# Taking sixteen experts in turn over four groups, and giving the rows before and after them to VectorE

## What is computed

```
h2   = rmsnorm(x1, g) * (1 + scale2) + shift2          # 320 x 2048
g    = top-1 of 4 expert groups;  e1, e2 = top-2 of the 4 experts of that group
out  = sum over the two:  weight * (silu(h2 @ w_gate[e]) * (h2 @ w_up[e])) @ w_down[e]
y    = rmsnorm(x1 + gate2 * out)
```

## Time and profile before

| | us |
|---|---|
| median of 3 runs | 1412.45 |
| range of the runs | 1411.66 to 1415.14 |
| the profiled execution's own time | 1411.79 |
| its span in the profile | 1409.8 |
| reciprocal root done, h2 begins | 745.8 |
| first expert's first product | 806.6 |
| last product of the last expert | 1355.9 |
| last VectorE instruction | 1405.1 |

### The profile page before, as it was taken

The page is one execution under the profiler, slowest core; times in us unless marked ns, Lnnn a source line. Parts: engine busy times, 40 slices in busy tenths (PEclk is TensorE's granted clock), DMA queues, the critical chain, the costliest instruction groups (busy, mean ns, idle before and its releaser), DMA issues.

```text
span 1409.8 us, 15927 instructions
## 1 busy us (share of the span) xinstructions
PE 1180.1 (84%) x6268; PEld 620.0 (44%) x6269; DVE 313.4 (22%) x624; ACT 200.7 (14%) x386; POOL 119.5 (8%) x129
## 2 busy tenths in 40 slices
PE   2678999999999999999991399999987877788740
PEld 0235665645445445444440344444644444444420
DVE  0101221142132232121109410111112111111128
ACT  2002111022022222100102000110211111111102
POOL 2010000000000001000007000000000000000016
PEclk9777999999999999999995599999999999999975
DMA  9987787766566439633512468877999999999953
GB/s 333 421 349 258 308 319 276 298 268 271 204 258 255 179 138 344 238 144 130 212 76 75 181 255 315 309 280 301 382 406 414 413 409 398 402 412 413 423 201 112
DMA packets 71717, 401.07 MB, mean 284 GB/s; under 512 B 6490, under 2 KB 6714, under 8 KB 39646
## 3 DMA queue, kind: packets, MB, share of 16 engines
q1 hardware_dynamic: 63216, 368.59, 66.8%
q0 software_dynamic: 6944, 23.99, 5.2%
q10 hardware_dynamic: 1520, 7.98, 1.4%
HBM read 394.85 MB, written 17.22 MB: 292 GB/s over the span
## 4 chain that ended last, share of the span: by engine, by line
PE 65%; DMA 26%; DVE 6%; issue 1%; ACT 1%; POOL 0%; SPq 0%; POOLq 0%; DVEq 0%
PE bank L825 20%; DMA arena<-in_w_up_dram 18%; PE bank L902 10%; PE bank L1175 8%; PE bank L829 5%; PE bank L817 5%; DMA arena<-in_w_ada_dram 5%; PE bank L1172 5%; PE bank L1198 4%; DMA arena<-in_w_gate_dram 2%; PE bank L1195 1%; PE bank L846 1%; DVE arena L1499 1%; PE bank L1036 1%; PE bank L1158 1%
## 5 line engine op out<-in xcount | busy, mean ns | idle before, releaser
L825 PE MATMUL bank<-arena 128*128 128x512 f32 x640 | 283.4, 596 | 0.0
L1172 PE MATMUL bank<-arena 128*64 128x256 f32 x1536 | 187.6, 403 | 58.3 <-DMA arena<-in_w_gate_dram 31.7
L825 PEld LDWEIGHTS bank<-arena 128*128 128x128 f32 x640 | 118.6, 190 | 137.7 <-issue 136.5
L1172 PEld LDWEIGHTS bank<-arena 128*64 128x64 f32 x1536 | 113.6, 145 | 137.0 <-DMA arena<-in_w_gate_dram 43.0
L902 PE MATMUL bank<-arena 128*128 128x320 f32 x512 | 143.2, 440 | 3.8 <-DVE arena L1274 3.8
L817 PE MATMUL bank<-arena 128*32 128x512 f32 x768 | 102.4, 674 | 45.0 <-DMA arena<-in_w_ada_dram 33.2
L902 PEld LDWEIGHTS bank<-arena 128*128 128x128 f32 x512 | 97.9, 192 | 51.1 <-issue 7.8
L1175 PE MATMUL bank<-arena 128*128 128x512 f32 x256 | 112.0, 598 | 6.9 <-issue 6.9
L1195 PE MATMUL bank<-arena 128*64 128x512 f32 x384 | 85.0, 595 | 6.0 <-DVE arena L1644 6.0
L1641 DVE SCALAR_TENSOR_TENSOR arena<-bank,arena 128x512 f32<-128x512 f32 x16 | 12.0, 751 | 346.5 <-PE bank L1172 232.4
L1175 PEld LDWEIGHTS bank<-arena 128*128 128x128 f32 x256 | 49.0, 192 | 68.6 <-issue 68.6
(11 more groups left out here) (320 smaller groups left out, 811.8 us busy)
## 6 DMA issues: line engine op xcount, KB each, us to landing
arena<-in_w_ada_dram SPq DMA_DIRECT2D x48, 2048.0 KB, 14.1
arena<-in_w_gate_dram SPq DMA_DIRECT2D x32, 2048.0 KB, 25.8
arena<-in_w_up_dram SPq DMA_DIRECT2D x32, 2048.0 KB, 27.2
arena<-in_w_down_dram SPq DMA_DIRECT2D x32, 2048.0 KB, 26.2
arena<-in_w_in_dram SPq DMA_DIRECT2D x20, 2048.0 KB, 7.7
arena<-in_w_out_dram SPq DMA_DIRECT2D x8, 2048.0 KB, 8.1
arena<-mod_final POOLq DMA_DIRECT2D x6, 1024.0 KB, 12.8
arena<-expert_rows SPq DMA_DIRECT2D x8, 512.0 KB, 7.7
```

The source lines that it names most:

```text
L825: mm(banks[j][:, :], lhsT=xT_[:, t, OFF[j]:OFF[j] + P], rhs=w_of(t), start=first and t == group[0], stop=final and t == group[-1])
L1172: last = mm(PB[bank][64 * h:64 * h + 64, 0:HALF], lhsT=XeT[:, t0 + t, 0:64], rhs=slots_w[slot][:, t, HALF * h:HALF * h + HALF], start=star ...
```

## The change

It has four parts.

1. **Order of the experts.** SP's loop takes expert 0 of each of the four groups, then expert 1 of each, and so on. Place i = 4e + g holds expert e of group g. The routing tables (top1, top2) are laid out in the same order. The loop body of SP now issues 24 transfers, and the first four experts are written out ahead of it.
2. **h2.** All three tiles are made by VectorE in the order sample, prompt 0, prompt 1 (`H2_ORDER`), with natural columns. ScalarE stores all three. GpSimd's two operations, ScalarE's scaling and the clearing of Xe are gone.
3. **Transposes.** The gathered rows now have natural columns, so each transpose (L1158) reads 128 columns that lie 16 apart.
4. **Last additions.** VectorE adds all 2048 columns, and GpSimd none.

```diff
-            expert(0, 0)
-            with sp.Fori(1, NE) as e:
-                expert(e, e)
+            for g in range(4):
+                expert(g, 0, g)
+            with sp.Fori(1, 4) as e:
+                for g in range(4):
+                    expert(g, e, 4 * e + g)
...
-            pool.wait_ge(s2_in, 64)
-            pool.wait_ge(h2_sample, 1)
-            o = by_t(h2p[2][0:DEC], out=True)
-            pool.tensor_tensor(o, o, by_t(a2b[0:DEC, 1, :]), ALU.mult).then_inc(h2_sample, 1)
-            pool.wait_ge(h2_sample, 2)
-            pool.tensor_tensor(o, o, by_t(s2b[0:DEC, 1, :]), ALU.add).then_inc(h2_sample, 1)
-            pool.wait_ge(h2_sample, 3)
-            pool.dma_start(h2_d[SEQ:TOK, :], h2p[2][0:DEC]).then_inc(h2_stored[2], 16)
-
-            pool.wait_ge(h2_ready, 2)
-            pool.memset(Xe, 0.0).then_inc(cleared, 1)
...
-            pool.wait_ge(cleared, 2)
+            pool.wait_ge(h2_ready, 3)
...
-            pool.wait_ge(tail_in, 48)
-            for j in range(3):
-                pool.wait_ge(x_in[j], 80)
-                add_rows(pool, step, j, slice(0, POOL_COLS)).then_inc(xf_pool, 1)
...
-            act.activation(by_t(h2p[2][0:DEC], out=True), by_t(x1[0:DEC, 2, :]), ACT.Copy, scale=st[0:DEC, 11:12]).then_inc(h2_sample, 1)
...
-            for j in range(2):
-                act.wait_ge(h2_ready, j + 1)
-                act.dma_start(h2_d[OFF[j]:OFF[j] + P, :], h2p[j]).then_inc(h2_stored[j], 16)
+            for k, j in enumerate(H2_ORDER):
+                act.wait_ge(h2_ready, k + 1)
+                act.dma_start(h2_d[OFF[j]:OFF[j] + NT[j], :], h2p[j][0:NT[j]]).then_inc(h2_stored[j], 16)
...
-                        last = tr(PB[2 + k][:, P * c:P * c + P], Xe[:, P * t:P * t + P], ident)
+                        last = tr(PB[2 + k][:, P * c:P * c + P], Xe.rearrange("q (p t) -> q t p", t=KT)[:, t, :], ident)
...
-            for j in range(2):
-                o = by_t(h2p[j], out=True)
-                step(V.scalar_tensor_tensor(o, by_t(x1[:, j, :]), col(9 + j), by_t(a2b[:, 0, :]), ALU.mult, ALU.mult))
-                V.tensor_tensor(o, o, by_t(s2b[:, 0, :]), ALU.add).then_inc(h2_ready, 1)
+            dve.wait_ge(slot_used[W1], 16)
+            for j in H2_ORDER:
+                n, b = NT[j], STREAM[j]
+                o = h2p[j][0:n]
+                step(V.scalar_tensor_tensor(o, x1[0:n, j, :], col(9 + j, 1, n), a2b[0:n, b, :], ALU.mult, ALU.mult))
+                V.tensor_tensor(o, o, s2b[0:n, b, :], ALU.add).then_inc(h2_ready, 1)
...
-            dve.wait_ge(h2_sample, 3)
             pick(0)
...
-                add_rows(V, step, j, slice(POOL_COLS, D)).then_inc(xf_ready, 1)
+                add_rows(V, step, j, slice(0, D)).then_inc(xf_ready, 1)
```

More of the change, by code:

```diff
@@ L240, in trunk @@
             sem, ("modq_in", "modf_ready", "modf_stored", "g1_in", "s2_in", "xr_in"))
-        outp_read, x1_ready, ssq2, rstd2, h2_ready, h2_sample, cleared = map(
-            sem, ("outp_read", "x1_ready", "ssq2", "rstd2", "h2_ready", "h2_sample", "cleared"))
+        outp_read, x1_ready, ssq2, rstd2, h2_ready, cleared = map(
+            sem, ("outp_read", "x1_ready", "ssq2", "rstd2", "h2_ready", "cleared"))
         h2_stored = [sem(f"h2_stored{j}") for j in range(3)]
         mod2_in, mod2T, wr_prod, wr_ready, x1Tp, x1T_out, lgp = map(sem, ("mod2_in", "mod2T", "wr_prod", "wr_ready", "x1Tp", "x1T_out", "lgp"))
-        gexp, gexp_in, mask_ready, rankp, tables, xf_ready, xf_pool = map(
-            sem, ("gexp", "gexp_in", "mask_ready", "rankp", "tables", "xf_ready", "xf_pool"))
+        gexp, gexp_in, mask_ready, rankp, tables, xf_ready = map(
+            sem, ("gexp", "gexp_in", "mask_ready", "rankp", "tables", "xf_ready"))
         Pm_ready, info, idx_ready, Xe_in, XTp, XeT_v, XeT_s = map(
@@ L271, in trunk @@
         ACT_TILES = (2, 5, 7, 10, 13, 15)
-        POOL_COLS = 768
+        H2_ORDER = (2, 0, 1)
         def add_rows(eng, step, j, cols):
@@ L280, in add_rows @@
             return eng.tensor_tensor(xj, xj, r0, ALU.add)
-        def by_t(a, out=False):
-            return a.rearrange("q (t p) -> q p t" if out else "q (p t) -> q p t", t=KT)
         def col_of(n):
@@ L363, in _, with expert @@
             sp.wait_ge(gmv_stored, 16)
-            def expert(e, i):
+            gate_of, up_of, down_of = (w[0].rearrange("(g e) k n -> g e k n", g=4) for w in (w_gate, w_up, w_down))
+            def expert(g, e, i):
+                first = isinstance(i, int) and i == 0
                 for s, kind, half in order:
-                    if not isinstance(i, int) or before_moe[s]:
+                    if not first or before_moe[s]:
                         sp.wait_ge(slot_used[s], i + before_moe[s])
-                    if isinstance(i, int) and s == W1:
+                    if first and s == W1:
                         sp.wait_ge(h2_stored[2], 16)
                     if kind == "d":
-                        src = w_down[0, bass.ds(e, 1)].rearrange("e (t p) n -> p (e t) n", p=P)[:, 2 * half:2 * half + 2, :]
+                        src = down_of[g, bass.ds(e, 1)].rearrange("e (t p) n -> p (e t) n", p=P)[:, 2 * half:2 * half + 2, :]
                         dst = slots_ada[s]
                     else:
-                        w = w_gate if kind == "g" else w_up
-                        src = w[0, bass.ds(e, 1)].rearrange("e (p t) n -> p (e t) n", t=KT)[:, 8 * half:8 * half + 8, :]
+                        w = gate_of if kind == "g" else up_of
+                        src = w[g, bass.ds(e, 1)].rearrange("e (p t) n -> p (e t) n", t=KT)[:, 8 * half:8 * half + 8, :]
                         dst = slots_w[s]
                     sp.dma_start(dst, src).then_inc(slot_in[s], 16)
-            expert(0, 0)
-            with sp.Fori(1, NE) as e:
-                expert(e, e)
+            for g in range(4):
[3 more added lines that the diff above has]
+                    expert(g, e, 4 * e + g)
             sp.wait_ge(tables, 1)
@@ L388, in _ @@
                 with sp.Fori(1, passes) as p:
-                    with sp.Fori(0, NE) as e:
-                        expert(e, NE * p + e)
+                    with sp.Fori(0, 4) as e:
+                        for g in range(4):
+                            expert(g, e, NE * p + 4 * e + g)
             sp.wait_ge(routed, 1)
@@ L799, in _ @@
                 act.wait_ge(xf_ready, j + 1)
-                act.wait_ge(xf_pool, j + 1)
                 act.activation(yrow[0:n, 2 * j + 1, :], x1[0:n, j, :], ACT.Square, accum_out=st[0:n, 80 + j:81 + j]).then_inc(fsq, 1)
@@ L1535, in g4, with in_turn @@
                 return a.rearrange("p j (g e) -> p j g e", g=4)
+            def in_turn(a):
+                return a.rearrange("p j (e g) -> p j g e", g=4)
             step(V.tensor_tensor(g4(prod), g4(el), grid(goh, 3), ALU.mult))
@@ L1544, in _ @@
             V.tensor_tensor(rt[:, :, 1:2], rt[:, :, 5:6], rt[:, :, 4:5], ALU.subtract).then_inc(gexp_in, 1)
-            step(V.tensor_tensor(g4(top1), grid(goh, 3), grid(eoh1, 2), ALU.mult))
-            step(V.tensor_tensor(g4(top2), grid(goh, 3), grid(eoh2, 2), ALU.mult))
+            step(V.tensor_tensor(in_turn(top1), grid(goh, 3), grid(eoh1, 2), ALU.mult))
+            step(V.tensor_tensor(in_turn(top2), grid(goh, 3), grid(eoh2, 2), ALU.mult))
             step(V.memset(top1[DEC:P, 2, :], 0.0))
```

2 lines of the change are left out of this document (removed).

## The result

| | before | after |
|---|---|---|
| median of four runs, us | 1413.76 | 1366.49 |
| range of the runs | 1411.66 to 1415.14 | 1362.26 to 1367.78 |
| the profiled execution's own time | 1411.79 | 1362.26 |
| its span | 1409.8 | 1360.6 |

The ratio is 0.9662, with a 95% interval of [0.9636, 0.9687]: 47 us less. The profiled execution of after is the fastest of its four, 4.2 us under their median, so the two profiles differ by 49.2 us where the medians differ by 47.3.

A forecast was written before the change was run, and what follows sets the result against it. TensorE was taken to bound the four large experts in a row, transfers the others. Order -30.6, h2 -12.5 and additions -4.1 sum to -47.2 from 1411.8; with the median's 0.66, 1365 us, range 1352 to 1382.

The forecast's parts named there:

- Order, -30.6 forecast: Expert stretch: large experts at places 0, 4, 8, 12 let transfers bound everything behind the first expert; -30.6 us.
- the two corrections: Expert stretch: 6 us for extra rows of three large experts, 2.6 us for the sum's shortfall on the kernel before.
- The rival without a gain from the order: Experts: transfers beside large experts stay at 0.81 share, so the order gives nothing; 1396 us, chance 0.08.
- The rule of the Trainium skill that the prediction weighed: Weight transfers: as a rival, HBM binds at 358 GB/s, an expert takes 37.2 us; 1430 us, chance 0.01.
- h2, -12.5 forecast: h2 to first routing operation: six natural-column operations and ten small ones, 15.9 us, replace 28.4 us; -12.5 us.
- The bound that was kept from the permuted rows: h2: if all six operations took permuted times (3.74 and 3.83), 22.7 + 1.8 us, a gain of only 3.9.
- the half rate that the prediction quoted: h2: scalar_tensor_tensor with two non-bf16 SBUF sources at half rate; three operations twice as long, 7 us more.
- Transposes, 0 forecast, up to 2.4 kept: Weight loads of columns 16 apart: taken as nothing; 75 ns more each would show 2.4 us around expert 0.
- Additions, -4.1 forecast: Kernel's end: VectorE alone takes 30.2 us for additions and finishes instead of 34.3; -4.1 us, within 1 us.
- The rival of 6 us at each change: TensorE switching between its two bodies: only the first change, behind expert 0, shows, 6 us; 1371 us, chance 0.10.
- Low clock: Large experts following waiting ones run at 1.2 GHz, 89.5 us each; +92 us, 1457 us, slower, chance 0.03.
- The range: Whole kernel: 1352 to 1382 us; upper end adds 5 for large experts, 2.4 transposes, 6 code, 4.5 weights.

The follow-up runs named there:

- the run with less weight: Kernel after, but from the second expert on only a quarter of w_down's second half is loaded, TensorE's work the same: 1321.56 us, ratio 0.9356.
- the run of the order alone: Kernel before with only the new order of the experts; h2, transposes and last additions as before: 1384.08 us, ratio 0.9809.
- the run with permuted columns: Kernel after with h2 on VectorE alone, but columns permuted and transposes reading adjacent ones: 1372.94 us, ratio 0.9739.
- the last runs: Kernel after with TensorE's two bodies exchanged in the program, 1356.62 us, and beside it the kernel after itself, 1365.67 us.
- the bodies exchanged: Kernel after with TensorE's large-expert body put ahead of the small one in the program, nothing else changed: 1356.62 us, ratio 0.9585.
- the two runs that begin with small experts: Kernel after with large experts at places 2, 6, 10, 14 (1353.79 us) or at 3, 7, 11, 15 (1358.84 us).

## Why the prediction came out as it did

**Order, -30.6 forecast, -29.0 measured.** The sum had two steps. The last slot of place 1 was to land 53.8 us after the first product (860.4 - 806.6). SP's loads in the profile after (start us, us for the pair) have it issued at some 837.9, and 7.3 us later is 53.7 after 791.51:

```profile
799.94 7.23 SPq L378 DMA_DIRECT2D arena<-in_w_gate_dram  x2
...
830.99 7.26 SPq L378 DMA_DIRECT2D arena<-in_w_down_dram  x2
```

From there each place was to take 32.95 us (32.34, with the 2.6 and the 6 us of the two corrections spread over fourteen). It took 33.08: (1311.75 - 3.5 - 845.2) / 14. So the form of the sum was right, and the remaining 1.6 us are 0.1 us for each place. That the transfers set the pace was the step on which all of it hung, and the run with less weight shows it. How much of the corrections is extra rows of large experts, and how much is shortfall, was not told apart. One sign came out otherwise: TensorE was to wait at small experts only, and it waits ahead of the large ones too (2.84, 2.68 and 3.11 us).

**The rate beside a large expert.** No row of before showed it. 413 GB/s from 921 to 966 shows that a busy TensorE doesn't slow the transfers. The rival without a gain from the order falls with it, and by the run of the order alone. The rule of the Trainium skill that the prediction weighed ("DMA: Bandwidth & Descriptors", section "Where 436 GB/s comes from") has the HBM side of one core bind at about 358 GB/s, which it reaches by dividing a stack's 716 by two cores. This launch is on one core, and its windows of 399 to 413 GB/s over 45 to 86 us lie above that share.

**h2, -12.5 forecast, -13.3 measured.** Six operations took 13.84 us where 14.1 was forecast, and the ten small ones 1.24 where 1.8 was: on the chain they pass at 0.12 us each, not 0.18. The bound that was kept from the permuted rows (3.74 and 3.83) is what the run with permuted columns measured, 3.65 to 3.78. A scalar_tensor_tensor over 2048 natural columns took 2.34 us, so the half rate that the prediction quoted from the Trainium skill ("Vector Engine (DVE) Microarchitecture Reference", section "Points that are easy to get wrong") isn't seen here either.

**Transposes, 0 forecast, up to 2.4 kept.** The set ahead of expert 0 takes 3.68 us in both kernels, the one inside it 1.97 instead of 1.91. A large expert is 0.05 us longer, beside transfers that end later anyway. The cost was put at nothing, and that held.

**Additions, -4.1 forecast, -5.1 measured.** The row that the term took, 2.35 us, is a scalar_tensor_tensor, and an addition takes 2.29 us. Three of them and their gaps are 6.86 (1326.62 to 1333.48) instead of 7.1, which is 0.7 in all; the finishes give the other 0.2. The 1.49 us of the earlier trace rows were read as a row without GpSimd. GpSimd's own operation began 0.05 us behind it:

```profile
1370.80 3.10 POOL L278 TENSOR_TENSOR arena<-arena 128x768 f32<-128x768 f32 x1 [11.04 <-DMA arena<-expert_rows]
```

The number was still that of an undisturbed operation: 2.29 x 1280 / 2048 is 1.43.

**Code switching.** The rival of 6 us at each change fell: between 823.83 + 13.99 and 837.76 there is no pause, and the later large experts wait for their weights. But the forecast took the pause ahead of the first product as given, since the change doesn't touch it. That kept the sum right, and the last runs showed that this pause hangs on where the first body stands in the program, and can be avoided.

**Low clock.** The windows have a clock of 0.96 to 1.00. One large expert's products take 29.46 us instead of 27.76 (granted clock 0.67 from 1052 to 1057, behind a wait of 2.68); these 1.7 us lie in TensorE's slack.

**The range.** The terms of its upper end add up to 1383, not 1382; nothing hangs on it.

## What to carry to other kernels

Where weights stream through a buffer of one stage and the stages differ in work, count what a run of heavy stages costs the transfers: spread among light ones they cost 28.9 us less here, with the same products and the same bytes. A second engine that shares an elementwise step isn't a gain by itself; compare both engines' rows beside each other with one engine's alone. Idle time that the profile puts down to nothing ("issue") is worth an experiment even where a change leaves it alone: exchanging the two bodies of a branch gave 9 us.

## What the runs showed of the hardware that was not expected

- **A pause that goes with a body's place in the program.** With a large expert first and the small body first in the program, TensorE stands 6.6 to 7.6 us ahead of its first product. With the large body first in the program, or a small expert first, it is 1.09 to 1.10. The Trainium skill, "Runtime: NRT & Kernel Launch", section "Instruction fetch mechanics", says that a taken branch to a target outside the fetched window has to fetch it before execution goes on; the pause agrees with that, but no run here shows the fetch itself. The rule alone isn't enough: the first entry into the body that stands second costs nothing where it comes later (831.22 with the bodies exchanged, right behind 817.29 + 14.00). A second pause, 3.60 us and 4.55 us, stands ahead of the second expert in the two runs that begin with small experts, and its cause is open.
- **GpSimd beside VectorE costs different amounts.** Over natural columns, 2.29 to some 3.0 us beside GpSimd's multiplications (1.3 times), and 1.49 to 2.97 beside its additions at the end of the kernel before (twice). It can also cost nothing: at the end, the operation that began 0.05 us ahead of GpSimd's took 1.49, and at h2 of the kernel before two permuted operations beside GpSimd's multiplication took 3.83 and 3.68 us (the latter from 753.33), where 3.65 to 3.78 is the time with GpSimd idle:

```profile
749.84 12.64 POOL L495 TENSOR_TENSOR arena<-arena 64x2048 f32<-64x2048 f32 x1 [4.51 <-ACT arena L762]
```

- **Longer weight loads that cost almost nothing.** Transposes with columns 16 apart load in 196 ns instead of 141, and sixteen of them add some 0.05 us to an expert.
